# A mixer and mixture-of-experts layer on one core: the first pieces of w_in taken in another order, and h2 formed by VectorE around the top-k steps

## The reference, cut to what matters

```python
h = rmsnorm(x, g_mix) * (1 + scale_m) + shift_m         # modulation: silu(c) @ w_ada + b_ada
z = h @ w_in                                            # 1024 -> pool 512|q 512|k 512|v 512|gate_a 1024|gate_b 1024
a = pool_mixer(u_pool) @ w_pa ; o = attention(q, k, v) @ w_pb
x = x + gate_m * ((sigmoid(ga) * a + sigmoid(gb) * o) @ w_out)
h = rmsnorm(x, g_ffn) * (1 + scale_f) + shift_f
logits = h @ w_router + b_router                        # 32 experts, the 4 largest of each token
x = x + gate_f * sum_e combine[:, e] * (swiglu(h @ w_up[e] + b_up[e]) @ w_down[e] + b_down[e])
y = rmsnorm(x, g_final)
```

## Time and profile before

| What | Value |
|---|---|
| median of 3 runs | 1161.99 us (1158.14 to 1162.92) |
| profiled execution, time | 1158.52 us |
| profiled execution, span | 1156.8 us, mean granted clock 0.981 |
| TensorE busy | 1056.0 us, 91% |
| VectorE, ScalarE, GpSimd busy | 334.7, 178.4, 61.9 us |
| DMA | 459.15 MB, mean 397 GB/s |

### The profile page before, as it was taken

The page is one execution under the profiler, slowest core; times in us unless marked ns, Lnnn a source line. Parts: engine busy times, 40 slices in busy tenths (PEclk is TensorE's granted clock), DMA queues, the critical chain, the costliest instruction groups (busy, mean ns, idle before and its releaser), DMA issues.

```text
span 1156.8 us, 13975 instructions
## 1 busy us (share of the span) xinstructions
PE 1056.0 (91%) x5704; PEld 520.2 (45%) x5704; DVE 334.7 (29%) x609; ACT 178.4 (15%) x323; POOL 61.9 (5%) x97
## 2 busy tenths in 40 slices
PE   6999999899999999999989898989898989898986
PEld 5987699834334343424343334343433343333322
DVE  5676877502313021202020202021212121212125
ACT  4453145501101010101010101010101010101011
POOL 5050000400000000000000000000000000000000
PEclk9999999899999999999999999999999999999999
DMA  9988977699999999999999999999999999999994
GB/s 309 377 240 329 388 286 316 276 367 425 420 403 429 426 429 427 429 428 429 427 429 429 429 428 428 430 427 429 428 429 427 429 429 429 428 427 423 422 420 195
DMA packets 58659, 459.15 MB, mean 397 GB/s; under 512 B 4805, under 2 KB 17161, under 8 KB 28057
## 3 DMA queue, kind: packets, MB, share of 16 engines
q1 hardware_dynamic: 57256, 455.12, 95.2%
q0 software_dynamic: 1168, 2.81, 1.0%
q10 hardware_dynamic: 192, 0.66, 0.2%
HBM read 456.99 MB, written 1.57 MB: 396 GB/s over the span
## 4 chain that ended last, share of the span: by engine, by line
PE 60%; DMA 33%; DVE 3%; SPq 2%; issue 1%; ACT 1%; POOL 0%; DVEq 0%; ACTq 0%
DMA ring<-in_w_down_dram 30%; PE ps L1842 17%; PE ps L1857 10%; PE ps L1779 6%; PE ps L1732 5%; PE ps L1743 5%; PE ps L1442 3%; DMA ring<-in_w_in_dram 2%; PE ps L1877 2%; PE ps L1772 1%; PE ps L1759 1%; DMA ring<-in_w_ada_dram 1%; PE ps L1497 1%; PE ps L1663 1%; PE ps L1498 1%
## 5 line engine op out<-in xcount | busy, mean ns | idle before, releaser
L1842 PE MATMUL ps<-ring,arena 128*64 128x512 f32 x1664 | 364.6, 594 | 17.4 <-DMA ring<-in_w_up_dram 17.3
L1857 PE MATMUL ps<-ring,arena 128*64 128x512 f32 x896 | 212.5, 630 | 50.1 <-DMA ring<-in_w_down_dram 50.1
L1842 PEld LDWEIGHTS ps<-ring,arena 128*64 128x64 f32 x1664 | 121.0, 137 | 244.3 <-issue 242.0
L1857 PEld LDWEIGHTS ps<-ring,arena 128*64 128x64 f32 x896 | 73.7, 145 | 188.6 <-issue 169.5
L1300 DVE TENSOR_TENSOR arena<-ps,arena 128x512 f32<-128x512 f32 x64 | 44.3, 692 | 297.4 <-PE ps L1743 297.4
L1281 DVE TENSOR_SCALAR arena<-ps 128x512 f32<-128x512 f32 x32 | 20.6, 686 | 258.9 <-PE ps L1842 220.2
L1779 PE MATMUL ps<-ring,arena 128*64 128x512 f32 x368 | 81.2, 594 | 1.0 <-DVE arena L1283 0.7
L1732 PE MATMUL ps<-arena 128*128 128x128 f32 x512 | 64.9, 286 | 1.7 <-DVE arena L1242 1.7
L1732 PEld LDWEIGHTS ps<-arena 128*128 128x128 f32 x512 | 62.9, 200 | 4.2 <-issue 4.2
L869 ACT ACTIVATE arena<-arena 128x512 f32<-128x512 f32 x32 | 19.6, 629 | 271.7 <-DVE arena L1281 271.7
L1269 DVE TENSOR_SCALAR arena<-arena,cur 128x64 f32<-128x64 f32 x64 | 11.9, 250 | 162.5 <-PE ps L1751 160.2
(11 more groups left out here) (277 smaller groups left out, 965.4 us busy)
## 6 DMA issues: line engine op xcount, KB each, us to landing
ring<-in_w_up_dram SPq DMA_DIRECT2D x127, 2048.0 KB, 26.9
ring<-in_w_down_dram SPq DMA_DIRECT2D x63, 2048.0 KB, 23.0
ring<-in_w_ada_dram SPq DMA_DIRECT2D x16, 1024.0 KB, 10.4
ring<-in_w_ada_dram SPq DMA_DIRECT2D x16, 512.0 KB, 9.8
ring<-in_w_in_dram SPq DMA_DIRECT2D x16, 512.0 KB, 9.6
ring<-in_w_in_dram SPq DMA_DIRECT2D x8, 1024.0 KB, 7.4
ring<-in_w_out_dram SPq DMA_DIRECT2D x4, 1024.0 KB, 6.6
ring<-in_w_pb_dram SPq DMA_DIRECT2D x2, 1024.0 KB, 8.4
```

Of the source, the lines that this page charges most:

```text
L1842: ins = mm(ps[CAP * a:CAP * a + CAP, n, :], xgT[:, h, kk, CAP * a:CAP * a + CAP], w[a][:, n * HALF:(n + 1) * HALF], start=False, stop=(kk ...
L1857: ins = mm(ps[CAP * a:CAP * a + CAP, YB + n, :], hT[:, f, CAP * a:CAP * a + CAP], w[a][:, n * HALF:(n + 1) * HALF], start=(f == 0), stop=( ...
```

## The change

1. The DMA of unit 1 moves ahead of those of `first(1)`. TensorE runs unit 1 right behind unit 0, then `first_rows(1)`, then unit 2 with `first_columns(1)` inside it. VectorE forms the remainders of units 1, 2 and 3 ahead of its copy of the rows.
2. x is loaded into `gtf`. ScalarE writes the transposed x straight into `x_chan`. The copy on GpSimd, `xT` and `xT_ready` go. GpSimd zeroes `bada` only after x has been read.
3. `h2a`, the scaling on ScalarE and the sums on GpSimd go. VectorE forms each quarter of h2 in one instruction from PSUM, two quarters behind `mask_ready` and two behind `oh_ready`. The scaled channels go to banks 2, 3, 5 and 7, those of x2T to banks 0, 1, 0 and 1, the second two behind the ranks.
4. TensorE gets three filler matmuls (`keep_busy`) ahead of the ranks and three behind the last `to_rows`. `up_bias(0)` moves ahead of the first gather, which waits for `x_back` 4. The clearing of `acc` on GpSimd waits for `cur_ready`.
5. The router accumulates both token groups in bank 6, which a matmul with a zeroed operand opens, and the sums of squares go to banks 0 and 1, one of them ahead of the last router step.

```diff
     first(0, 0, 1)
     unit(0, 2, 0)
+    unit(1, 2, 1)
     first(1, 3, 4)
-    unit(1, 2, 1)
     unit(2, 5, 0)
...
-            sp.dma_start(x[:, 0, :], A_x_prompt[0]).then_inc(L["x0"], 16)
-            sp.dma_start(x[:, 1, :], A_x_sample[0]).then_inc(L["x1"], 16)
+            sp.dma_start(gtf[:, 0, :], A_x_prompt[0]).then_inc(L["x0"], 16)
+            sp.dma_start(gtf[:, 1, :], A_x_sample[0]).then_inc(L["x1"], 16)
...
             root(1)
+            pool.wait_ge(xn_ready, 2)
+            pool.wait_ge(xT_t, 2)
             link(nc.gpsimd.memset(bada[:, :, :], 0.0))
...
-            pool.wait_ge(xT_read, 2)
-            pool.wait_ge(xn_ready, 2)
-            nc.gpsimd.tensor_copy(x_chan, xT).then_inc(xT_ready, 1)
...
-            for k_, (n, t) in enumerate(NT):
-                c = slice(n * HALF, (n + 1) * HALF)
-                pool.wait_ge(bc_read, 2)
-                pool.wait_ge(h2a_ready, k_ + 1)
-                nc.gpsimd.tensor_tensor(h2[:, t, c], h2a[:, t, c], h2[:, t, c], ALU.add).then_inc(h2_ready, 1)
...
             pool.wait_ge(x2_t, 4)
+            pool.wait_ge(cur_ready, 1)
             nc.gpsimd.memset(acc, 0.0).then_inc(acc_zero, 1)
...
             for k, (n, t) in enumerate(NT):
-                act.wait_ge(af_t, k + 1)
-                act.wait_ge(root_ready, 3)
-                nc.scalar.activation(h2a[:, t, n * HALF:(n + 1) * HALF], ps[:, 2 + 2 * t + n, :], ACT.Copy,
-                                     scale=rstd[:, t:t + 1]).then_inc(h2a_ready, 1)
...
+                if k == 2:
+                    act.wait_ge(top_ready, 1)
+                    for g in range(2):
+                        nc.scalar.activation(rt[:, g, 1, :], rt[:, g, 0, :], ACT.Exp,
+                                             bias=misc[:, 4 + g:5 + g]).then_inc(e_ready, 1)
                 act.wait_ge(x2_t, k + 1)
-                nc.scalar.activation(x[:, t, n * HALF:(n + 1) * HALF], ps[:, 2 + 2 * t + n, :],
+                nc.scalar.activation(x[:, t, n * HALF:(n + 1) * HALF], ps[:, X2_BANK[k], :],
                                      ACT.Copy).then_inc(x_back, 1)
...
             for q in range(1, 4):
-                early_rests(3 * q - 2)
+                if q == 1:
+                    early_rests(1, 2, 3)
+                else:
+                    early_rests(3 * q - 2)
                 first_rows(q)
-                early_rests(3 * q - 1, 3 * q)
+                if q > 1:
+                    early_rests(3 * q - 1, 3 * q)
...
+            def h2_out(k):
+                n, t = NT[k]
+                c = slice(n * HALF, (n + 1) * HALF)
+                dve.wait_ge(af_t, k + 1)
+                V.scalar_tensor_tensor(out=h2[:, t, c], in0=ps[:, AF_BANK[k], :], scalar=rstd[:, t:t + 1],
+                                       in1=h2[:, t, c], op0=ALU.mult, op1=ALU.add).then_inc(h2_ready, 1)
+
+            h2_out(0)
+            h2_out(1)
...
+            h2_out(2)
+            h2_out(3)
             dve.wait_ge(e_ready, 2)
...
                 project(3 * q)
+                if q == 0:
+                    pe.wait_ge(xr_ready, 2)
+                    cleared(2)
+                    project(1)
                 if q < 3:
                     first_rows(q + 1, 0)
                     first_rows(q + 1, 1)
                 if q == 0:
-                    pe.wait_ge(xr_ready, 2)
-                    cleared(2)
+                    cleared(4)
+                    project(2, lambda: first_columns(1))
+                    continue
...
+                    pe.wait_ge(zeroed, 1)
+                    mm(ps[:, 6, 0:2 * E], ident[:, :], woT[:, 0, 0:2 * E], start=True, stop=False)
...
-            for n, t in NT:
-                to_rows(x_chan, n, t).then_inc(af_t, 1)
-            for k, (n, t) in enumerate(NT):
-                pe.wait_ge(h2a_ready, k + 1)
-                to_rows(x2T, n, t).then_inc(x2_t, 1)
+            for k in range(4):
+                to_rows(x_chan, k, AF_BANK[k]).then_inc(af_t, 1)
+            pe.wait_ge(mean_ready, 3)
+            for k in range(2):
+                to_rows(x2T, k, X2_BANK[k]).then_inc(x2_t, 1)
+            keep_busy(3, 4)
 
             pe.wait_ge(mask_ready, 1)
...
+            for k in range(2, 4):
+                pe.wait_ge(x_back, k - 1)
+                to_rows(x2T, k, X2_BANK[k]).then_inc(x2_t, 1)
+            keep_busy(3, 4)
...
-                up_bias(R)
+                if second_half is None:
+                    up_bias(R)
...
             pe.wait_ge(h2_ready, 2)
-            pe.wait_ge(x_back, 3)
+            pe.wait_ge(x_back, 4)
+            up_bias(0)
             gather(0, 0, FIRST[0])
```

More of the change, by code:

```diff
@@ L311, in layer_kernel @@
         bc_done, bc_read = sem("bc_done"), sem("bc_read")
-        xT_t, xT_read, xT_ready = sem("xT_t"), sem("xT_read"), sem("xT_ready")
+        xT_t, xT_read = sem("xT_t"), sem("xT_read")
         cols_done, cols_read = sem("cols_done"), sem("cols_read")
@@ L658, in _ @@
                 act.wait_ge(L[f"x{t}"], 16)
-                nc.scalar.activation(xn[:, t, :], x[:, t, :], ACT.Square,
+                nc.scalar.activation(xn[:, t, :], gtf[:, t, :], ACT.Square,
                                      accum_out=ssq[:, t:t + 1]).then_inc(ssq_ready, 1)
@@ L734, in _ @@
                 .then_inc(bias_copied, 1)
-            act.wait_ge(xT_ready, 1)
             z_out(3)
@@ L990, in _ @@
                 dve.wait_ge(root_ready, t + 1)
-                V.tensor_scalar(xn[:, t, :], x[:, t, :], rstd[:, t:t + 1], None, ALU.mult).then_inc(xn_ready, 1)
+                V.tensor_scalar(xn[:, t, :], gtf[:, t, :], rstd[:, t:t + 1], None, ALU.mult).then_inc(xn_ready, 1)
             def mod_rows(m):
@@ L1200, in _ @@
                 if j == 0:
-                    dve.wait_ge(xT_ready, 1)
+                    dve.wait_ge(xT_read, 2)
                     dve.wait_ge(m_ready, KB)
@@ L1217, in _ @@
             for t in range(2):
-                ins = V.scalar_tensor_tensor(out=rt[:, t, 0, :], in0=ps[:, 6 + t, 0:E], scalar=rstd[:, t:t + 1],
+                ins = V.scalar_tensor_tensor(out=rt[:, t, 0, :], in0=ps[:, 6, E * t:E * t + E], scalar=rstd[:, t:t + 1],
                                              in1=cst[:, t, :], op0=ALU.mult, op1=ALU.add)
@@ L1433, in first_columns, with project @@
                 ins.then_inc(modT_done, 1)
-            def project(n):
+            def project(n, between=None):
                 cc, q = UNITS[n]
@@ L1461, in project @@
                     for b, a in blocks:
+                        if (b, a) == (1, 0) and between is not None:
+                            between()
                         product(b, a, early_top, hT_top)
@@ L1510, in _ @@
                 for j in range(KB):
-                    ins = tp(ps[:, 2 + 2 * t + j // 4, (j % 4) * P:(j % 4 + 1) * P], x[:, t, j * P:(j + 1) * P], ident[:, :])
+                    ins = tp(ps[:, 2 + 2 * t + j // 4, (j % 4) * P:(j % 4 + 1) * P], gtf[:, t, j * P:(j + 1) * P], ident[:, :])
                 ins.then_inc(xT_t, 1)
@@ L1669, in router @@
                     pe.wait_ge(cols_read, 4)
+                    pe.wait_ge(zeroed, 1)
+                    mm(ps[:, 6, 0:2 * E], ident[:, :], woT[:, 0, 0:2 * E], start=True, stop=False)
                 pe.wait_ge(x2T_ready, j + 1)
                 for t in range(2):
-                    ins = mm(ps[:, 6 + t, 0:E], x2T[:, j, t * P:(t + 1) * P], wrtA[:, t, j, :],
-                             start=(j == 0), stop=(j == KB - 1))
+                    ins = mm(ps[:, 6, E * t:E * t + E], x2T[:, j, t * P:(t + 1) * P], wrtA[:, t, j, :],
+                             start=False, stop=(j + t == KB))
                 if j == KB - 1:
@@ L1690, in _, with to_rows @@
                     router(j - 1)
+            pe.wait_ge(sqs_ready, KB - 2)
+            mm(ps[:, 0, 0:2], sqs[:, 0:P], ones[:, 0:2], start=True, stop=False)
             router(KB - 1)
[L1692 removed]
+            mm(ps[:, 1, 0:2], sqs[:, P:TOK], ones[:, 0:2], start=True, stop=False)
             pe.wait_ge(sq_ready, KB)
             for t in range(2):
[L1695 to L1696 removed]
+                ins = mm(ps[:, t, 0:2], sq[:, 3, t * P:(t + 1) * P], ones[:, 0:2], start=False, stop=True)
             ins.then_inc(logit_done, 1)
[L1699 removed]
+            def to_rows(src, k, bank):
+                n, t = NT[k]
                 for j in range(4 * n, 4 * n + 4):
[L1701 removed]
+                    ins = tp(ps[:, bank, (j % 4) * P:(j % 4 + 1) * P], src[:, j, t * P:(t + 1) * P], ident[:, :])
                 return ins
```

29 lines of the change are left out of this document (8 added, 21 removed).

## The result

| What | Before | After |
|---|---|---|
| median of the runs of this comparison | 1158.14 us (1157.37 to 1162.92, 7 runs) | 1152.35 us (1151.41 to 1153.73, 7 runs) |
| ratio, 95% interval | | 0.9945, 0.9934 to 0.9957 |
| profiled execution, time | 1158.52 us | 1152.35 us |
| profiled execution, span | 1156.8 us | 1150.5 us |

The kernel became 0.55% faster. So the gain is 5 to 6.4 us where 4.4 us were forecast. The time was off by 5.2 us all the same, since the forecast started from a base that was too high.

A forecast was written before the change was run, and what follows sets the result against it. DMA was taken to bound the last three quarters, compute the start of the stream. 2.4 + 2.0 = 4.4 us off the profiled 1158.5 us gave 1154.1, lifted 3.5 us to 1157.6, stated as 1157.5 us; range 1152.5 to 1162.0 us.

The forecast's parts named there:

- Part A: First 40 us, parts 1 and 2 of the change: unit 3 starts at 32.1 instead of 34.5 us, gaining 2.4 us.
- the 1.85 us: VectorE's remainder of unit 1 if it lies behind whole GpSimd instructions, instead of the 1.6 us taken.
- the lower bound of 0.9 us: Least gain of part A, if the clock falls all the same and unit 1 keeps 4.60 us.
- rival 2: A late transfer (relative-position bias, a piece of w_ada) absorbs part A; gain 2.0 us, 1160.0 us; chance 0.14.
- Part B: Router to first expert block, parts 3 to 5: first w_up block at 230.2 instead of 232.24 us, gaining 2.0 us.
- The sum from the sums to the block: Time from the router's sums (`logit_done`) to the first block of w_up: 13 us instead of 14.7.
- The upper bound of 3.0 us for part B: The 2.8 us hole in the stream plus 0.2 us of the router; a still earlier start gains no more.
- the DMA hole: DMA engines busy 0.29 of the time from 234 to 238 us, so standing still for 2.8 us.
- Rival 1: The clock falls in the filler stretch or at the gather; gain 1.3 us in all, 1160.7 us; chance 0.15.
- Rival 3: Fillers cost more than they bring, TensorE needing over 17.5 us to the first block; 2.1 us slower, 1164.1 us; chance 0.06.
- Rival 4: More than priced: parts A and B reach 3.0 us each, or the stream gains too; 6 to 7 us, 1155.5 us; chance 0.15.

The follow-up runs named there:

- order_only: The kernel before with the new order of the first pieces (part 1) but x still in its old buffer: 1156.99 us, ratio 0.9992.
- b_only: The kernel before with parts 3 to 5 of the change alone: 1154.96 us, ratio 0.9963.
- after_again: The kernel after, unchanged, measured and profiled a second time: 1152.78 us, ratio 0.9957 against the kernel before.
- old_filled: The kernel before with nine filler matmuls where TensorE waits for the mask and six where it waits for the one-hots: 1158.52 us, ratio 1.0005.
- old_fitted: The kernel before with five filler matmuls ahead of the ranks and three behind them: 1156.20 us, ratio 0.9986.
- a_only: The kernel before with parts 1 and 2 of the change alone: 1156.99 us, ratio 0.9986.
- pool_load: The kernel after with four unused GpSimd additions of 512 columns beside the top-k steps: 1155.92 us, ratio 0.9974 against the kernel before.
- fill_more: The kernel after with nine filler matmuls in place of the second three, 2.6 us more on TensorE: 1155.43 us, ratio 0.9980 against the kernel before.
- rows_early: The kernel after with VectorE's copy of the rows ahead of its share of unit 3: 1152.97 us, ratio 0.9956 against the kernel before.
- no_fill: The kernel after without its two groups of three filler matmuls: 1152.94 us, ratio 0.9942 against the kernel before.

## Why the prediction was wrong

**The base.** The largest error is not in the kernel. The sum gave 1154.1 us from the profiled execution's 1158.52, and I lifted it by 3.5 us to the median of three runs, 1161.99. In this comparison the kernel before had a median of 1158.14 us, and beside the experiments 1157.7 to 1158.8 us over 15 to 23 runs each. The three runs were high by 3.9 us. Of the 5.2 us between forecast and time, 3.9 are this step: the lift from the profiled execution to the median of three. That the profiled execution was a typical one was luck: in order_only it lies 4.4 us above the median of its kernel, in b_only 2.4 us below.

**Part A: 2.4 us forecast, 0.7 us at the router.** The sums are 1.0 us early, but 0.3 us of that belongs to part 5 of the change: from VectorE's last step on x2T to the sums it takes 1.95 us (214.62 to 216.57 us), and 2.24 before. The numbers up to 30 us came as worked out: unit 1 at 22 us, the stall of 0.7 us, unit 3 2.2 us early where the clock holds. One of them came by luck: VectorE was to end unit 1's remainder at 21.8 us and bind, but it took 2.44 us for the two remainders from 18.80 us on and was done at 21.24; TensorE worked without a gap up to 21.97, on unit 0 and the bank clearing. So neither the 1.6 us nor the 1.85 us priced for that remainder was met; it took 1.2. Two things were missing. In the profiled execution of after the clock fell from 30.4 to 33.8 us, which cost 1.1 us against after_again and which the lower bound of 0.9 us covered. And the advance was capped later by transfers, rival 2, which I gave 0.14: the bias transfer at 72 us and the pieces of w_ada up to 141 us. In the profile of after, already late by the clock, that took only 0.3 us more; in after_again, with the clock held, 2.1 us at unit 3 became 0.9 at the router, part 5's 0.3 taken off. How much of part A reaches the router is not firm: against the sums of old_filled and old_fitted in place of before it would be 1.6 and 1.5 us and not 0.7. I had named the transfer and not worked out when it lands. Its issue waits for the landing of unit 15, which the change does not move, and its landing 11.9 us behind the issue leaves 1.6 us.

**Part B: 2.0 us forecast, 4.4 us measured.** That is 4.1 us from the sums to the block and part 5's 0.3 us ahead of the sums, which the forecast put at 0.2. The mask 3.5 us after the sums, comparisons at 0.22 us, h2 quarters at 0.7 us, fillers of 1.30 us, gather of 2.1 us, and TensorE's own queue as the path: all right. The sum from the sums to the block was 13.1 us and took 10.52 us, 2.6 us less. The mis-sized term is the transposes: 3.04 + 1.4 us forecast, 2.68 us measured. I took the 3.04 us from the earlier trace rows, where the clock was at 1.2 GHz, as the cost of that work. The stretch of the kernel before and its slow part:

```profile
216.00:222.00 6.00, 5.99 (x39) 5.99 (x40) 3.40 (x8) 5.61 (x12) 3.22 (x4) 0.72 0.81 306
218.00:221.00 3.00, 3.00 (x16) 3.00 (x15) 2.24 (x7) 2.63 (x6) 2.08 (x3) 0.50 0.78 259
```

The stretch 216 to 222 us has a clock of 0.72 in the profiles of before and order_only and of 1.00 in those of a_only, old_filled and old_fitted, all five with the old order; it is 1.00 in all nine with the new one. The rest is 0.3 us in the ranks, 0.2 in the second transposes, 0.2 in the bias matmuls and 0.1 in ScalarE's copy. With the full clock's 2.68 us in its place the sum would have been 11.3 us. The forecast also starts this sum at 217.1 us, 0.2 us too early (the sums at 217.60 less part 5's 0.3 are at 217.3), so of the 2.6 us 2.4 show in part B.

How the 4.1 us divide: 1.5 us is the clock at the gather and the bias matmuls (old_fitted). The other 2.6 us, by subtraction, is the order of the work with GpSimd's sums gone; additions put back beside the top-k steps take 1.9 us of it away again (pool_load), and no run takes the last 0.7 us apart. The fillers have no part in it that shows, although such fillers are worth 1.5 us in the old order.

**The upper bound of 3.0 us for part B failed.** I argued that a start earlier than the DMA hole is long would find a stream without a gap and gain no more. fill_more and the constant 158.8 us show that TensorE binds from the block to the turn of the chain, and the hole is only where the ring shows that it waits for TensorE. The number stood in my own rows: 145.27 us busy of 146. I read them as "both are full" and left open which engine the other waits for.

**The stream.** From the turn to the last landing the profile of before took 730.6 us and that of after 729.2. The change does not touch that stretch, and the fourteen executions lie between 729.1 and 731.2 us, with old and new blocks among each other. So 1.4 us of the 6.3 us between the two spans is this variation and not the change.

**Rivals.** Rival 1 (the clock falls in the new block) held in none of nine executions. Rival 2 holds in part: with the clock's fall it took 1.7 of the 2.4 us of part A in the profile of after. Rival 3 did not come, since TensorE needed 10.5 us, not over 17.5. Rival 4 (1155.5 us, from the same high base) comes nearest to the result, with its gain of 6 to 7 us, but for another reason: part A gave less than it says, and part B more than its bound.

## What to carry to other kernels

Price each instruction by a row at the clock level that it will have, and carry both levels: one profile's fall of the clock is not a property of the work. When two engines are both full, ask which of them would be idle if the other were faster; a hole in the transfers behind a full ring is TensorE's limit, and here an earlier start was worth all of it. For each moved piece of work look for the next transfer whose issue doesn't move with it, and add its landing time. And don't lift a forecast onto the median of three runs: here they were 3.9 us off, two thirds of the gain. Forecast the difference, and put what the base may be off by into the range.

## What the runs showed of the hardware that was not expected

Where the clock falls differs between executions of one kernel: from 30 to 34 us it was 0.57 in one profile of the kernel after and 1.00 in the other. It still follows the kernel in frequency. With the old order of pieces it fell between 26 and 30 us in three of four executions, each costing 1.35 us at unit 3 (37.4 against 36.05 us), and with the new one, which has no wait for unit 1, near 30 us in one of ten. Between 122 and 127 us it fell in rows_early and order_only, behind 2.0 and 2.1 us of idle time, and not in old_filled behind 2.19 us. Before the gather it fell in all three executions of the old block without fillers, where TensorE had idled 2.3 to 3.3 us for the mask and 1.65 us for the one-hots, and in none of the eleven others, with idle times of at most 0.95 us (no_fill) or 1.6 us (pool_load). The Trainium skill (TensorE: Matmul & The Clock Gate, "Part 1") has the monitor run free of the program, so that the place of a fall can differ between executions. The two profiles of the kernel after agree, with 0.57 and 1.00.

The last of eight bias transfers issued by GpSimd landed 11.6 to 12.1 us after its issue in the seven executions whose chain shows it; from 60 to 72 us the memory moved 290 to 307 GB/s in them.
